# Three unsplit products instead of five at four stage starts, and GpSimd's low parts in 528-wide operations

## The reference

```
xn = rms_norm(x, attn_norm);  z = xn @ w_in                      # q, k, v, lru_x, lru_gate, merge gates
attn_branch = attention(q, k, v) @ w_attn_out
lru_branch  = (rg_lru(conv(lru_x)) * gelu(lru_gate)) @ w_lru_out
x = x + (g_a * attn_branch + g_b * lru_branch) @ w_o
gate, up = split(rms_norm(x, ffn_norm) @ w_gate_up)
x = x + (silu(gate) * up) @ w_down
```

## Time and profile before

| | |
|---|---|
| runs | 1732.95 us median of 3 (1731.3 to 1734.54) |
| profiled execution, its own time | 1729.97 us |
| its span | 1728.2 us |
| TensorE clock granted, mean | 0.98 of full |
| PE busy | 1643.9 us, 95% of the span |
| PEld, DVE, POOL, ACT busy | 90%, 62%, 60%, 36% |

### The profile page before, as it was taken

How to read it: one execution, slowest core, us unless ns; L and a number is a source line. 1 busy time by engine, 2 the same in 40 slices (tenths; PEclk the granted TensorE clock), 3 DMA queues, 4 the chain that set the end, 5 groups by cost and what they waited for, 6 DMA issues and landing times. The chain is left out here.

```text
span 1728.2 us, 29284 instructions
## 1 busy us (share of the span) xinstructions
PE 1643.9 (95%) x11338; PEld 1556.1 (90%) x11338; DVE 1069.8 (62%) x1613; ACT 624.5 (36%) x1308; POOL 1030.8 (60%) x703
## 2 busy tenths in 40 slices
PE   5999999999999999799798997999999999999999
PEld 4999998988989898699797986999999999898999
DVE  5867673964747565757789778333333334959585
ACT  4355533234343424424224333333333333323242
POOL 4656552222222121479786727777777777989896
PEclk9999999999999999999998998999999999999999
DMA  4111112233122131254342511222233222272634
GB/s 163 38 61 61 61 52 101 66 88 101 55 82 78 62 101 56 95 216 177 132 150 75 176 73 43 81 79 95 75 122 128 85 78 75 105 283 99 258 139 153
DMA packets 72765, 182.13 MB, mean 105 GB/s; under 512 B 14704, under 2 KB 26416, under 8 KB 72000
## 3 DMA queue, kind: packets, MB, share of 16 engines
q1 hardware_dynamic: 51376, 159.13, 25.7%
q10 hardware_dynamic: 21264, 21.27, 4.1%
HBM read 131.36 MB, written 49.28 MB: 105 GB/s over the span
## 5 line engine op out<-in xcount | busy, mean ns | idle before, releaser
L581 PE MATMUL bank<-xh,wsh 128*128 128x264 f32 x2178 | 623.7, 286 | 13.4 <-DVE xl L1500 5.2
L581 PE MATMUL bank<-xh,wsl 128*128 128x264 f32 x2178 | 620.8, 285 | 0.0
L581 PE MATMUL bank<-xl,wsh 128*128 128x264 f32 x2178 | 620.1, 285 | 0.0
L581 PEld LDWEIGHTS bank<-xh,wsh 128*128 128x128 f32 x2178 | 411.7, 189 | 15.1 <-issue 14.2
L581 PEld LDWEIGHTS bank<-xl,wsh 128*128 128x128 f32 x2178 | 411.8, 189 | 0.2
L581 PEld LDWEIGHTS bank<-xh,wsl 128*128 128x128 f32 x2178 | 411.7, 189 | 0.0
L581 PE MATMUL bank<-acth,wh 128*128 128x352 f32 x1008 | 337.7, 335 | 8.8 <-issue 5.7
L581 PE MATMUL bank<-acth,wl 128*128 128x352 f32 x1008 | 328.1, 325 | 0.0
L581 PE MATMUL bank<-actl,wh 128*128 128x352 f32 x1008 | 326.7, 324 | 0.0
L499 POOL TENSOR_SCALAR wh<-wraw 128x512 fp32r<-128x512 f32 x104 | 85.1, 819 | 388.0 <-PE bank L581 375.7
L549 POOL TENSOR_TENSOR wsl<-praw,wsh 128x512 fp32r<-128x512 f32 (+1 forms) x158 | 235.4, 1490 | 97.0 <-ACT wsh L1157 96.6
(11 more groups left out here) (165 smaller groups left out, 2489.9 us busy)
## 6 DMA issues: line engine op xcount, KB each, us to landing
praw<-in_weights SPq DMA_DIRECT2D x34, 1024.0 KB, 4.9
wraw<-in_weights SPq DMA_DIRECT2D x52, 512.0 KB, 3.3
h_scratch<-ev SPq DMA_DIRECT2D x44, 264.0 KB, 2.1
acc<-h_scratch SPq DMA_DIRECT2D x4, 2112.0 KB, 12.9
ev<-x_scratch SPq DMA_DIRECT2D x6, 1056.0 KB, 5.1
spare<-x_scratch SPq DMA_DIRECT2D x6, 1056.0 KB, 5.0
praw<-in_weights SPq DMA_DIRECT2D x8, 768.0 KB, 5.1
x_scratch<-ev SPq DMA_DIRECT2D x5, 1056.0 KB, 4.0
```

Source lines behind the costliest of these rows:

```text
L581: return nc.tensor.matmul(*args, **kw)
```

## The change

In stages 1, 4, 5 and 6 the products 4 and 5 of the first pair become split ones, so that 2, 3 and 6 stay unsplit. There GpSimd makes low part 4 at r = 2 and 5 at r = 3, still ahead of `w_sum(p, 3)`, and adds `w_low(p, 4)` and `w_low(p, 5)`; in stages 0, 2 and 3 the low parts move behind `w_sum(p, 3)`. Each of GpSimd's low parts of X is made by an operation of 528 columns for each chunk, in place of one of 2112 (1584 at t = 6). In GATE_UP the plain pair computes its products in another order (the second half of the columns earlier) with other banks, and the norm, the gates and X's sums follow in a new order; X's high and low parts 4 and 5 change places. `combine_gated` waits for the residual rows only where they are read. The diff:

```diff
--- before.py
+++ after.py
@@ -152,14 +152,14 @@
 PHASE_FIRST = tuple(sum(PAIRS[:t]) for t in range(PHASES + 1))
 N_PAIRS = PHASE_FIRST[PHASES]
 PLAIN = PHASE_FIRST[GATE_UP]
-PLAIN_ORDER = ((0, 0, 0), (0, 1, 0), (0, 0, 1), (1, 0, 0), (0, 1, 1), (1, 1, 0), (1, 0, 1), (1, 1, 1))
-PLAIN_BANKS = {(0, 0): 2, (1, 0): 0, (0, 1): 4, (1, 1): 6}
-FP32 = ((0, 1, 2, 3, 4, 5, 6),) + ((2, 3, 4, 5, 6),) * (PHASES - 1)
+PLAIN_ORDER = ((0, 0, 0), (0, 0, 1), (0, 1, 1), (0, 1, 0), (1, 0, 1), (1, 1, 1), (1, 0, 0), (1, 1, 0))
+PLAIN_BANKS = {(0, 0): 2, (1, 1): 0, (0, 1): 4, (1, 0): 6}
+FP32 = ((0, 1, 2, 3, 4, 5, 6), (2, 3, 6), (2, 3, 4, 5, 6), (2, 3, 4, 5, 6)) + ((2, 3, 6),) * 3
 X_FIRST = tuple(f + (f == PLAIN) for f in PHASE_FIRST[:PHASES])
 BANKS = ((0, 1), (4, 5), (2, 3), (6, 7), (0, 1), (4, 5), (6, 7))
-POOL_LOWS = ((4, 5), (4, 5), (4, 5), (0, 4, 5), (4, 5), (4, 5), (4, 5))
+POOL_LOWS = ((4, 5), (4, 5), (4, 5), (0, 5, 4), (4, 5), (4, 5), (4, 5))
 DVE_LOWS = ((0, 1, 2, 3, 6), (0, 1, 2, 3, 6), (0, 1, 2, 3, 6), (1, 2, 3, 6)) + ((0, 1, 2, 3, 6),) * 3
-HIGHS = ((0, 1, 2, 4, 5, 3, 6), (0, 1, 4, 5, 2, 3, 6), (0, 1, 2, 5, 4, 3, 6), (0, 1, 4, 2, 5, 3, 6)) + ((0, 1, 4, 5, 2, 3, 6),) * 3
+HIGHS = ((0, 1, 2, 4, 5, 3, 6), (0, 1, 4, 5, 2, 3, 6), (0, 1, 2, 5, 4, 3, 6), (0, 1, 5, 2, 3, 4, 6)) + ((0, 1, 4, 5, 2, 3, 6),) * 3
 MERGED_LRU = 3 * PAIRS[LRU_OUT]
 X_LOADED = {ATTN_OUT: 32, DOWN: 64, DOWN + 1: 96, DOWN + 2: 128}
 
@@ -250,7 +250,7 @@
     for t in range(1, PHASES):
         f = X_FIRST[t]
         if t == GATE_UP:
-            order = {(f, 0): (2, 5), (f, 1): (3,), (f, 4): (6,)}
+            order = {(f, 0): (5, 2), (f, 1): (3,), (f, 2): (4,), (f, 4): (6,)}
         elif t == OUT:
             order = {(f - 1, 0): (0,), (f - 1, 1): (1,), (f, 0): (2, 5), (f, 1): (4, 3), (f, 4): (6,)}
         else:
@@ -552,8 +552,9 @@
             def part_low(t, k):
                 pool.wait_ge(xhi_done, nth_high(t, k))
                 n = chunks_of(t)
-                nc.gpsimd.tensor_tensor(xl[k][:, 0:n, :], x_part(t, k), xh[k][:, 0:n, :].bitcast(f32), ALU.subtract)\
-                    .then_inc(plow_done, 1)
+                for c in range(n):
+                    i = nc.gpsimd.tensor_tensor(xl[k][:, c, :], x_part(t, k)[:, c, :], xh[k][:, c, :].bitcast(f32), ALU.subtract)
+                i.then_inc(plow_done, 1)
 
             for p in range(N_PAIRS):
                 if p == PLAIN:
@@ -564,11 +565,14 @@
                         part_low(t, 0)
                     if r in (0, 1, 2):
                         w_sum(p, r)
-                    if r == 3 and p == X_FIRST[t]:
-                        part_low(t, 4)
-                        part_low(t, 5)
+                    if p == X_FIRST[t] and not in_fp32(p, 4) and r in (2, 3):
+                        part_low(t, r + 2)
                     if r == 4:
                         w_sum(p, 3)
+                        if p == X_FIRST[t]:
+                            for k in POOL_LOWS[t][-2:]:
+                                if in_fp32(p, 4):
+                                    part_low(t, k)
                     if not in_fp32(p, r):
                         w_low(p, r)
 
@@ -784,7 +788,7 @@
                 elif t == OUT:
                     pe.wait_ge(merged, MERGED_LRU + {0: 8, 4: 16, 5: 15}[k])
                 elif t == GATE_UP:
-                    pe.wait_ge(n2_done, {0: 4, 4: 12, 5: 16}[k])
+                    pe.wait_ge(n2_done, {0: 8, 4: 16, 5: 12}[k])
                 else:
                     pe.wait_ge(xs_in, X_LOADED[t])
 
@@ -797,7 +801,7 @@
             def bank_free(p, r, n):
 
                 if p == PLAIN + 1:
-                    pe.wait_ge(plain_done, (3, 5, 1, 7)[r] + n)
+                    pe.wait_ge(plain_done, (3, 1, 5, 7)[r] + n)
                 elif p:
                     pe.wait_ge((c11_done, c12_done, u2_done, c21_done)[r], 2 * nth(p) - 1 + n)
 
@@ -848,16 +852,13 @@
                         pe.wait_ge(acc_copied, 2)
                         pe.wait_ge(u2_done, last)
                     elif r == 1:
-                        pe.wait_ge(c11_done, last)
-                    elif r == 2:
                         sumsq2(0)
                         pe.wait_ge(c12_done, last)
+                    elif r == 2:
+                        sumsq2(1)
+                        pe.wait_ge(c11_done, last)
                     elif r == 3:
-                        sumsq2(1)
-                        pe.wait_ge(c21_done, last)
-                    elif r == 4:
                         pe.wait_ge(std2_done, 4)
-                    elif r == 6:
                         pe.wait_ge(c22_done, last)
                     for n in range(2):
                         out = bank[PLAIN_BANKS[m, h] + n][:, 0:QB]
@@ -1165,7 +1166,7 @@
                     act.wait_ge(acc_copied, 1)
                     act.wait_ge(merged, MERGED_LRU + {0: 8, 4: 16, 5: 15}[k])
                 elif t == GATE_UP:
-                    act.wait_ge(n2_done, {0: 4, 4: 12, 5: 16}[k])
+                    act.wait_ge(n2_done, {0: 8, 4: 16, 5: 12}[k])
                 else:
                     act.wait_ge(xs_in, X_LOADED[t])
                 if t:
@@ -1237,12 +1238,13 @@
                     for n in range(2):
                         act.wait_ge(ssall_done, 2 * h + n + 1)
                         f(ssum[:, piece(h, n)], bank[6 + n][:, 0:QB], ACT.Sqrt, scale=1.0 / D, bias=EPS).then_inc(std2_done, 1)
-                for h in range(2):
+                for h in (1, 0):
                     for n in range(2):
-                        act.wait_ge(plain_done, (1, 5)[h] + n)
+                        act.wait_ge(plain_done, (5, 1)[h] + n)
                         f(gate(h, n), gate(h, n), ACT.Silu).then_inc(plain_silu, 1)
-                    x_high(GATE_UP, h)
-                x_high(GATE_UP, 4)
+                    if h:
+                        x_high(GATE_UP, 0)
+                        x_high(GATE_UP, 1)
 
             w_after, x_after = w_high_after(), x_high_after()
             act.wait_ge(unit_done, EARLY_N)
@@ -1524,7 +1526,7 @@
                         dve.wait_ge(acc_copied, 1)
                     dve.wait_ge(merged, MERGED_LRU + (8, 15, 15, 16)[i])
                 elif t == GATE_UP:
-                    dve.wait_ge(n2_done, (8, 16, 16, 16)[i])
+                    dve.wait_ge(n2_done, (8, 12, 12, 16)[i])
                 else:
                     dve.wait_ge(xs_in, X_LOADED[t])
                 if i:
@@ -1543,7 +1545,7 @@
             def n2(kh, h):
 
                 dve.wait_ge(rstd2_done, 2 * h + 2)
-                dve.wait_ge(mm_done, ended(PLAIN, ((1, 4), (5, 7))[kh][h]))
+                dve.wait_ge(mm_done, ended(PLAIN, ((3, 2), (7, 5))[kh][h]))
                 for c in range(KQ * kh, KQ * kh + KQ):
                     dve.wait_ge(x1_stored, 16 * (c // 2 + 1))
                     stt(acc[:, c, toks(h)], acc[:, c, toks(h)], vt[:, c, V_G2:V_G2 + 1], ssum[:, toks(h)],
@@ -1557,24 +1559,25 @@
                         .then_inc(plain_done, 1)
 
             def plain_pair():
-                rstd2(0)
-                rstd2(1)
+                for j in range(4):
+                    rstd2(j)
+                n2(0, 1)
                 n2(0, 0)
-                rstd2(2)
-                rstd2(3)
-                plain_out(0, 0, 3)
-                n2(0, 1)
                 x_sum(GATE_UP, 0)
-                plain_out(1, 0, 5)
-                n2(1, 0)
-                plain_out(0, 1, 6)
+                plain_out(0, 1, 4)
+                plain_out(1, 1, 5)
                 part_low(GATE_UP, 1)
-                plain_out(1, 1, 7)
                 n2(1, 1)
                 x_sum(GATE_UP, 1)
+                plain_out(0, 0, 6)
+                plain_out(1, 0, 7)
+                dve.wait_ge(plain_silu, 2)
+                dve.wait_ge(plain_done, 4)
+                V.tensor_tensor(u4(0), u4(0), gate(1), ALU.mult).then_inc(h1_done, 1)
+                x_sum(GATE_UP, 2)
+                n2(1, 0)
                 dve.wait_ge(plain_silu, 4)
                 dve.wait_ge(plain_done, 8)
-                V.tensor_tensor(u4(0), u4(0), gate(1), ALU.mult).then_inc(h1_done, 1)
                 V.tensor_tensor(u2(0), u2(0), gate(0), ALU.mult).then_inc(h0_done, 1)
 
             def add_square(j):
@@ -1602,6 +1605,10 @@
                         dve.wait_ge(v_done, 3 * nres)
                     stt(u4(par, n), bank[BANKS[1][n]][:, 0:QB], scale, u2(par, n), ALU.mult, ALU.add).then_inc(u4_done, 1)
 
+            def rows_in(p):
+                for b, n in res_loads(p).items():
+                    dve.wait_ge(res_in[b], n)
+
             def combine_gated(p, r):
 
                 t = phase_of(p)
@@ -1612,8 +1619,8 @@
                 m, h = ((1, 1), (0, 0), (0, 1), (1, 0))[r - 3]
                 done = (c22_done, c11_done, c12_done, c21_done)[r - 3]
                 a = res[b][:, m, :]
-                for bb, n in res_loads(p).items():
-                    dve.wait_ge(res_in[bb], n)
+                if r == 4:
```

(3 more changed lines are left out.)

## The result

The changed kernel takes 1753.41 us (median of 4 runs, 1752.72 to 1754.99) against 1732.12 us for the kernel before on the same chip (4 runs, 1731.14 to 1734.54). The ratio on record is 1.0135, 95% interval 1.0117 to 1.0154; the quotient of the two medians alone is 1.0123, inside it. So the change is slower, by 21.3 us by the medians and by some 23 by the ratio, where 1752 us had been forecast. The profiled execution has a span of 1751.3 us, 23.1 more than before, at a mean granted clock of 0.976 (0.983 before).

A forecast was written before the change was run, and what follows sets the result against it. TensorE, busy 95%, was taken to bound the kernel. Stages 4, 5, 6, 1, 0, 2, 3 sum 7.5 + 7.5 + 6.5 + 1.5 - 1.5 + 0 - 2 = +19.5 us, forecasting 1752 us on the median, range 1739 to 1763.

The forecast's parts named there:

- The wait on ScalarE: Stages 4 to 6, 1: w_high(p, 5) waits for w_sum(p, 3), holding x_high(t, 2) and VectorE; +7.5, +7.5, +6.5, +1.5 us.
- contention of `part_low(t, 2)`: VectorE at the stage start: part_low(5, 2) takes about 2.4 us instead of 6.17, GpSimd's weights adding up to 1.3.
- the clock: Product 6 behind a hole of 3 to 5 us runs at a low clock, adding 0 to 1.7 us.
- the direct gain of 0.55 per product: TensorE: a four-chunk product takes 2.95 us split against 3.5 unsplit; eight products together 4 us, where TensorE isn't waiting.
- Stage 1: Product 6 +2.9 to +4.1 us late, residual rows read later give back 2.0: +1.5.
- Stages 0, 2, 3: w_sum(p, 3) moves ahead of the low parts, removing holes before product 5 in stages 0 and 2: -1.5, 0 and -2 us.
- what is late next is pair p+1: Stages 0, 2, 3: the next pair's w_sum and w_low stand behind the low parts; stage 0 hole 9.5 instead of 10.75.
- The price of the short operations: GpSimd: four 528-wide operations take 5.2 us against 4.9 to 5.0 for one; VectorE gets in after at most 1.3.
- The moved sums win: Rival: holes at the starts of stages 0, 2 and 3 all go, -10, 1723 us; chance 7%.
- Half of it: Rival: GpSimd is cut into less, stages 0, 2, 3 give 9 to 14: +6 to +11, 1738 to 1744 us; 15%.
- Worse: Rival: slow clock behind each new hole and full contention, +28 to +35, 1761 to 1768 us; 18%.
- The wait doesn't bite: Rival: ScalarE's wait for w_sum(38, 3) ends by 1580, leaving the 4 us and removed holes, 1720 us; 2%.

The follow-up runs named there:

- b3: Kernel before with only the change's FP32 line, so products 4 and 5 of pairs 4, 34, 38 and 42 become split: 1759.51 us, 1.0173.
- a3: Whole change with w_high(p, 5) and w_high(p + 1, 0) on ScalarE moved behind product 1, after x_high(t, 2), in the four stages: 1740.43 us, 1.0066.
- b1: Whole change with GpSimd's low parts of X in single operations of 2112 (1584) columns again: 1749.07 us, 1.0124 of the kernel before.
- c1: Change with five unsplit products, low parts ahead of w_sum(p, 3) in stages 1, 4, 5, 6, and single-operation low parts: 1718.25 us, 0.9949 of the kernel before.
- c3: c1 with stage 2's order put back as in the kernel before: 1723.47 us, 0.9967 of the kernel before.
- b2: Kernel before with one edit, GpSimd's low parts in 528-wide operations: 1746.42 us, 1.0103.
- c2: a4 with low parts in single operations; products 4 and 5 stay split: 1725.11 us, 0.9988 of the kernel before.
- a4: a3 with GpSimd making w_low(p, 4) and w_sum(p, 3) between the two low parts: 1741.58 us, 1.007 of the kernel before.
- a2: Change with five unsplit products and low parts ahead of w_sum(p, 3) in stages 1, 4, 5, 6; short operations kept: 1727.38 us, 1.0004 of the kernel before.

## Why the prediction was right

**The sum.** Forecast +19.5 on the profiled execution; its seven stages show +25.1, and 2.0 us came off ahead of them, so +23.1. The median rose by 21.3. That the total came within 2 us of 1752 is in part luck: stages 1 and 4 to 6 lost 33.7 us for 23.0, stages 0, 2 and 3 gave 8.6 for 3.5, and the 2.0 ahead of them were not in the sum. What was right is the sign and the mechanism, not the size of each stage.

**The wait on ScalarE** was right in mechanism and in time. For stage 5 the prediction has, on the old axis, `w_sum(38, 3)` done at 1586.5, `w_low(38, 4)` at 1587.8, TensorE at product 4 at 1585.1; less the shift of 4.06 the trace has 1586.0, 1587.2 and 1585.0. Then it has product 6 6.2 to 8.9 us late; it is 1606.45 - 4.06 - 1594.19 = 8.2 late. b3 and a3 show it from both sides.

**Two terms were sized too low.** The first is contention of `part_low(t, 2)`: "about 2.4 instead of 6.17" was the sign named, with up to 1.3 more from GpSimd's weights in the sum, and it took 4.71 in stage 5 and 4.72 in stage 4, each time behind GpSimd's weight operations, which start just as ScalarE is released. The second is the clock, counted at "0 to 1.7" and put into +7.5 at its low end. The windows of stage 5 in the changed kernel are product 4, product 5, product 6 and the next pair (the last three columns are the granted clock, DMA's share, GB/s):

```profile
1591.32:1595.73 4.41, 4.41 (x24) 4.10 (x24) 2.00 (x1) 4.41 (x4) 4.41 (x4) 0.68 0.00 0
1599.40:1604.09 4.69, 4.69 (x24) 4.48 (x24) 4.55 (x6) 0.00 (x0) 3.11 (x3) 0.64 0.01 3
1606.45:1611.93 5.48, 5.48 (x18) 4.43 (x19) 5.48 (x7) 2.02 (x2) 2.71 (x2) 0.69 0.00 0
1611.58:1632.45 20.87, 20.87 (x172) 20.84 (x171) 11.97 (x18) 4.52 (x9) 12.78 (x9) 1.00 0.84 317
```

and of products 4 and 6 of the same pair before:

```profile
1584.86:1588.42 3.56, 3.56 (x18) 3.04 (x17) 3.39 (x6) 0.00 (x0) 3.56 (x2) 1.00 0.90 299
1594.19:1597.99 3.80, 3.80 (x18) 3.28 (x19) 3.80 (x6) 2.48 (x2) 3.80 (x2) 1.00 0.00 0
```

0.68, 0.64 and 0.69 are stretches partly at the lower of the two levels, 1.2 GHz, behind the holes. Product 6 took 5.48 instead of 3.80: 1.7 lost, as at stage 4, in full and not in part, and 8.2 + 1.7 = 9.9 is the table's stage 5. At stage 6 product 6 took 5.62 instead of 2.91, at 0.50. And product 4, which the split was to bring from 3.5 to 2.95, took 4.4 from its first record to its last, where the unsplit one had taken 3.7: the direct gain of 0.55 per product became a loss. Stages 4, 5 and 6 came out at 29.3 instead of 21.5 (by unrounded entries). The prediction's sign for a low clock, the size of the hole just ahead, did not hold: a hole of 3.71 left product 6 at 3.80 in b1, holes of 2.06 and 2.04 gave 3.80 and 5.49 in c1 and c3. What decides whether the clock falls is not shown.

**Stage 1**, +4.4 for +1.5: product 6 was 4.9 late, above 2.9 to 4.1; another 1.1 came behind it, with a hole of 0.58 before pair 5; the rows gave back 3.2, not 2.0; and a smaller hole stayed before pair 6 (2.70), with its product 0 at a granted clock of 0.65, so that this pair took 1.5 longer, which the sum did not have.

**Stages 0, 2, 3.** The step "what is late next is pair p+1" held. In stage 0 the eight operations and VectorE's share took 15.6 for 16.5, a hole of 8.16 for 9.5, and -1.4 for -1.5. In stage 2 low parts end at 935.0, some 2 us earlier than counted, hence -2.2. In stage 3 -5.0 stands for -2, within the ends given; c1 and c3 show that the same code gives either.

**The price of the short operations** is the step that failed without moving the result. "The form itself costs 0.3 for each low part" is about right for an undisturbed one: eight took 10.14 in stage 4, the two single ones of the earlier trace rows in stage 2 9.72. But its gain, "VectorE gets in", is at the same time its price, since GpSimd has the work that TensorE waits for. In the forecast this entered only as VectorE's share in single sums. b2 measures it at 18 us on the old order, b1 at about 2 in the new one.

**The rule weighed in the prediction**, from the Trainium skill, SBUF — State Buffer, § Who interferes with whom, says that an operation of VectorE with two SBUF inputs and one of GpSimd that reads SBUF keep each other out for a whole instruction. The traces agree: the same eight operations took 10.14, 12.32 and 15.86 us with none, one and five of VectorE's two-input operations in between, and VectorE's 2112 columns took 3.3 to 3.5 beside short operations and 6.2 to 6.8 beside long ones. Shorter operations changed who was blocked: the low parts rose from 11.43 to 15.86 as VectorE's single waits fell.

**Rivals.** *The moved sums win* did not happen, as the low parts never fitted into two products; c1 shows that what stages 0, 2 and 3 can give is 7 us, of which 3 need not come. *Half of it* came near in its own part: stages 0, 2 and 3 gave 8.6 us where it had 9 to 14, with GpSimd cut into by 0.9 us less than counted in stage 0 and 1.7 in stage 2; the other stages outweighed it. *Worse* had the slow clock behind each new hole, which came in most of them, but not the gain of stages 0, 2 and 3. *The wait doesn't bite* is excluded by a3 and b3.

**Open.** The clock's share was read from windows, not taken away by a run, and no run shows why the clock falls behind one hole and not behind an equal one. So the two orders of stage 3 were not steered by an experiment either. Whether the split products would pay with nothing in their way is not shown: c2 still has GpSimd's holes.

## What to carry to other kernels

Before an operation is placed in an in-order queue, write down what stands behind it and what it waits for: here one 0.63 us copy that waited 16 us held up an eviction and two other engines, and moving two such copies gave 12 of 23 us back. Making a unit of work cheaper on the bounding engine is worth only what its operands' makers can follow: the shorter product was to be worth 0.55 us and put 12 us of low parts onto the path. Where two engines keep each other out instruction by instruction, short operations are a choice of who waits: cutting up the one that the bounding engine waited for cost 18 us here (b2). Before two kernels are compared to within a few us, their products behind holes are compared first: one at a lower clock cost 1.5 to 2.7 us here by itself, and 3 where it tipped an order.

## What the runs showed that was not expected

- One edit, the width of GpSimd's operations, cost 18 us (b2), 14 us (a4 against c2), 9 us (a2 against c1, 3 of them from stage 3's two cases, as in a4 against c2) or about 2 us (the change against b1), by what VectorE was free to do meanwhile.
- The same product behind the same hole took 3.80 us in one kernel and 5.48 in the other, at granted clocks of 1.00 and 0.69. The next engine's start 1.2 us later turned two separate operations into a block of 10.23 us in identical code, and 3 us were gone (c1, c3).
- A split product behind a hole of 2.24 us took 4.4 us from first record to last, against 3.7 for the unsplit one it replaced, at a granted clock of 0.68.
